# Two blocks on one core: all eight banks in one turn, ScalarE for the high parts of every dense weight unit, another place for the third FFN's second unit

## What is computed

```
for li in 0, 1:                                   # first block, two layers
    z = rms(x) @ w_in                              # 7756 columns: an mLSTM, a top-k attention, a differential attention
    merged = sum over 3 branches of sigmoid(gate) * (y_branch @ w_branch)
    x = x + merged @ w_out                         # 1024 x 1024
    x = x + (silu(rms(x) @ w_gate) * (rms(x) @ w_up)) @ w_down        # hidden 2816: first and second FFN
x = x + retention(rms(x) @ ret_w_in) @ ret_w_out   # ret_w_out: 2048 x 1024
x = x + (silu(rms(x) @ w_gate) * (rms(x) @ w_up)) @ w_down            # hidden 3584: third FFN
x = x + conv(rms(x) @ conv_w_in) @ conv_w_out
x = x + sum over 8 experts of gate_e * FFN_e(rms(x))                  # top 2 of 8, hidden 3584 each
out = rms(x) * g
```

## Time and profile before

| what | us |
|---|---|
| three runs | 2657.6, 2659.8, 2660.11 (median 2659.8) |
| the profiled execution | 2658.11 |
| its span, first to last instruction | 2656.3 |
| TensorE matmuls busy | 2592.8 (98%) |
| VectorE busy | 1803.0 (68%) |
| ScalarE busy | 1226.1 (46%) |
| GpSimd busy | 218.8 (8%), all of it L2251 but for 0.2 |

### The profile page before, as it was taken

How to read it: one execution, slowest core, us unless ns; L and a number is a source line. 1 busy time by engine, 2 the same in 40 slices (tenths; PEclk the granted TensorE clock), 3 DMA queues, 4 the chain that set the end, 5 groups by cost and what they waited for, 6 DMA issues and landing times.

```text
span 2656.3 us, 29239 instructions
## 1 busy us (share of the span) xinstructions
PE 2592.8 (98%) x11620; PEld 1989.4 (75%) x11620; DVE 1803.0 (68%) x1953; ACT 1226.1 (46%) x1423; POOL 218.8 (8%) x104
## 2 busy tenths in 40 slices
PE   8999999999999999999999998999999999999997
PEld 5455578865555888977788897878787888888886
DVE  3754555447445554745655567999999999999996
ACT  2233220023323102363100346777787877777775
POOL 0000023200000332000433100000000000000000
PEclk9999999999999999999999998999999999999999
DMA  6342455534334555545555455999999989999995
GB/s 214 129 154 100 158 192 189 170 110 137 127 113 170 193 190 173 184 157 175 175 190 190 143 176 181 375 325 381 320 379 325 377 324 376 325 355 347 354 345 188
DMA packets 273636, 610.13 MB, mean 230 GB/s; under 512 B 10476, under 2 KB 47522, under 8 KB 273338
## 3 DMA queue, kind: packets, MB, share of 16 engines
q1 hardware_dynamic: 273466, 607.67, 64.6%
HBM read 606.58 MB, written 1.05 MB: 229 GB/s over the span
## 4 chain that ended last, share of the span: by engine, by line
PE 90%; DVE 6%; ACT 3%; issue 1%; DMA 0%; SPq 0%; DVEq 0%; ACTq 0%
PE bank L467 87%; DVE split L1625 4%; PE bank L709 1%; PE bank L497 1%; ACT split L1195 1%; ACT parts L1195 0%; ACT xs L1195 0%; DVE tmp L1674 0%; DVE parts L1686 0%; ACT pbuf L1195 0%; DMA pbuf<-in_gain_rows 0%; DVE parts L1613 0%; ACT L1195 0%; ACT halves L1195 0%; DVE ybuf_tmp_high L1639 0%
## 5 line engine op out<-in xcount | busy, mean ns | idle before, releaser
L467 PE MATMUL bank<-split,parts 128*128 128x512 f32 (+1 forms) x6432 | 1463.3, 388 | 5.7 <-DVE split L1625 3.1
L467 PEld LDWEIGHTS bank<-split,parts 128*128 128x128 f32 x6432 | 1189.4, 188 | 247.3 <-issue 4.0
L1625 DVE TENSOR_TENSOR split<-ring,split 128x2048 fp32r<-128x2048 f32 x444 | 1020.4, 2344 | 81.9 <-POOL split L2251 60.9
L1195 ACT ACTIVATE split<-ring 128x2048 fp32r<-128x2048 f32 x344 | 659.6, 1921 | 187.0 <-PE bank L467 187.0
L467 PE MATMUL bank<-ring,xnT 128*128 128x512 f32 (+2 forms) x896 | 367.6, 567 | 0.0
L2251 POOL TENSOR_SCALAR split<-ring 128x2048 fp32r<-128x2048 f32 x100 | 218.6, 2187 | 1265.2 <-PE bank L467 1035.9
L467 PEld LDWEIGHTS bank<-ring,xnT 128*128 128x128 f32 x896 | 169.4, 190 | 180.0 <-issue 178.9
L1195 ACT ACTIVATE parts<-bank 128x512 fp32r<-128x512 f32 x128 | 68.8, 590 | 327.4 <-PE bank L709 327.4
L1639 DVE TENSOR_TENSOR halves<-ring,halves 128x1024 fp32r<-128x1024 f32 x96 | 116.4, 1224 | 84.1 <-ACT halves L1195 83.5
L1195 ACT ACTIVATE halves<-ring 128x1024 fp32r<-128x1024 f32 x96 | 101.3, 1059 | 153.9 <-PE bank L467 153.9
L1686 DVE TENSOR_TENSOR parts<-bank,parts 128x512 fp32r<-128x512 f32 x128 | 82.4, 686 | 124.9 <-ACT parts L1195 124.9
(11 more groups left out here) (260 smaller groups left out, 1861.1 us busy)
## 6 DMA issues: line engine op xcount, KB each, us to landing
ring<-in_moe_w_gate SPq DMA_DIRECT2D x112, 1024.0 KB, 8.0
ring<-in_moe_w_up SPq DMA_DIRECT2D x112, 1024.0 KB, 7.5
ring<-in_moe_w_down SPq DMA_DIRECT2D x112, 1024.0 KB, 7.5
ring<-in_w_gate_up SPq DMA_DIRECT2D x44, 1024.0 KB, 5.8
ring<-in_w_in SPq DMA_DIRECT2D x40, 1024.0 KB, 7.1
ring<-in_ret_w_in SPq DMA_DIRECT2D x24, 1024.0 KB, 5.1
ring<-in_w_down SPq DMA_DIRECT2D x22, 1024.0 KB, 5.1
ring<-in_w_in SPq DMA_DIRECT2D x20, 880.0 KB, 6.5
```

The lines of the kernel that those rows point to most:

```text
L467: return nc.tensor.matmul(o, l, r, start=first, stop=final, **kw)
L1195: return nc.scalar.activation(out, in_, func, **kw)
L1625: V.tensor_tensor(split[:, split_place(m), 1, :], ring[:, n % RING, :], split[:, split_place(m), 0, :].bitcast(F32), ALU.subtract).then_in ...
```

## The change

- ScalarE makes every high part, in `ffn_act`, in a written order: before a group's SiLU as many as the gate's units free, after it as many as the group's other units free. GpSimd's program goes.
- In the layers the early high and low parts follow 2, 1, 1 halves, the fourth unit last.
- In the third FFN and the experts the places are 3, 0, 1, 2 in turn. The third FFN's second unit thus goes where the first two of the retention's last four halves lay; it waits for these two and is made before the product ends. VectorE makes its low part between the addition of x's second half and the low parts of that half. Halves after the third FFN are numbered two places on.
- `to_x_split`, the transposes around it and the second filler take their banks from `ALL`; afterwards `LOW`'s counter is set so that the gate's banks aren't those emptied last.
- The last `combine` is preceded by a filler of three.

```diff
@@ split_place
-            return (3, 2, 0, 1)[(m - (DEPTH * layer_splits if m < dense_splits else dense_splits)) % SPLITS]
+            return (3, 0, 1, 2)[(m - (DEPTH * layer_splits if m < dense_splits else dense_splits)) % SPLITS]
@@ halves: place of half h
+            return (h if h < LAYER_HALVES + RET_HALVES else h + 2) % HALVES
@@ norm_transposes, input_split
-                filler(1)
+                filler(1, ALL)
@@ turn_residual
-                turn_input(x, (2 * h, 2 * h + 1), HIGH)
+                turn_input(x, (2 * h, 2 * h + 1), HIGH if h else ALL)
@@ to_x_split
-                bs = [fill(LOW) for _ in range(4)]
+                bs = [fill(ALL) for _ in range(4)]
...
+                for start in LOW:
+                    if bs[2] not in (LOW * 2)[start:start + 2] and bs[3] not in (LOW * 2)[start:start + 2]:
+                        turn[LOW] = start
@@ turn_merged; turn_o likewise
-                    turn_input(xs, (2 * h, 2 * h + 1), HIGH if h else ALL)
+                    turn_input(xs, (2 * h, 2 * h + 1))
@@ combine
+                filler(3 if ends else 0, LOW)
@@ ffn_act
                 highs(gain, pairs=(2, 3))
+                highs_to(SPLITS)
                 roots(xsum[:, 2, :], xsum[:, 1, :])
                 eng.wait_ge(rstd_dve.sem, act.next(rstd_dve))
-                for i in range(len(groups) + 1):
+                read = 0
+                for i in range(len(groups)):
                     if i:
-                        hidden_high(groups[i - 1][1], i == len(groups))
-                    if i < len(groups):
-                        gated(groups[i][1], normed=False)
+                        hidden_high(groups[i - 1][1], False)
+                    highs_to(read + ups[i] + SPLITS)
+                    gated(groups[i][1], normed=False)
+                    read += 2 * ups[i] + (downs[i - 1] if i else 0)
+                    highs_to(read - (1 if i + 1 == len(groups) else 0) + SPLITS)
+                hidden_high(groups[-1][1], True)
@@ layer, ScalarE (VectorE the same with half_lows and weights_low)
-                for _ in range(EARLY):
-                    half_highs(1)
+                for n in (2, 1, 1):
+                    half_highs(n)
                     expert_high(1, layer_splits * li)
+                expert_high(EARLY - 3, layer_splits * li)
@@ third FFN, ScalarE
             half_highs(8)
+            expert_high(1, first)
+            for h in range(LAYER_HALVES + RET_HALVES - HALVES, LAYER_HALVES + RET_HALVES - 2):
+                sig, value = half_read[h]
+                eng.wait_ge(sig.sem, value)
+            expert_high(1, first)
             ffn_act(groups2, G_FFN0, first)
@@ third FFN, VectorE
             weights_low(1)
-            to_ffn(G_FFN0)
-            weights_low(1)
+            to_ffn(G_FFN0, 1)
@@ to_ffn
                     add_to_x(BY_HALF[2 * h:2 * h + 2])
+                    weights_low(units if h else 0)
                     lows(gain, pairs=(2 * h, 2 * h + 1))
@@ GpSimd
-                    nc.gpsimd.tensor_scalar(split[:, split_place(m), 0, :], ring[:, n % RING, :], 1.0, 0.0, ALU.mult,
-                                            ALU.add).then_inc(high_made.sem, high_made.tick())
```

More of the change, by code:

```diff
@@ L46 @@
 LAYER_HALVES = DEPTH * KT
+RET_HALVES = 8 * 2 + 8 * 4 + 2 * KT
 EARLY = 4
@@ L344, in place_half @@
             else:
-                whole = [halves[:, h % HALVES, i, :] for i in range(2)]
+                whole = [halves[:, half_place(h), i, :] for i in range(2)]
             return [w.rearrange("p (k c) -> p k c", k=KT) for w in whole] if by_column else whole
@@ L499, in transposes, with filler @@
                 last_bank[0] = b
-            def filler(products):
+            def filler(products, pool):
                 if products:
-                    b = fill(LOW)
+                    b = fill(pool)
                     for _ in range(products):
@@ L509, in norm_transposes @@
             def norm_transposes(late=False, idle=(0, 0)):
-                filler(idle[0])
+                filler(idle[0], LOW)
                 if not late:
@@ L520, in norm_transposes @@
                                "act" if kp % 2 == 0 else "dve")
-                filler(idle[1])
+                filler(idle[1], ALL)
             def give_low(b):
@@ L535, in input_split @@
             def input_split():
-                filler(5)
+                filler(5, LOW)
                 eng.wait_ge(xs_act.sem, pe.next(xs_act))
@@ L1055, in o_ready @@
                 if k == 4:
-                    turn_o(RH - 1, HIGH)
+                    turn_o(RH - 1)
                     point("o turned")
@@ L1300, in hidden_high, with ffn_act, highs_to @@
                          view=lambda b: b[:, 0:n].rearrange("p (f t) -> p f t", t=P))
-            def ffn_act(groups, gain):
+            def ffn_act(groups, gain, first):
+                ups = [group_units(i, groups)[0] for i in range(len(groups))]
+                downs = [n // 256 for _, n in groups]
+                total = units_of(groups)
+                def highs_to(count):
+                    count = first + min(count, total)
+                    expert_high(max(0, count - nth_split[0]), first)
                 highs(gain, pairs=(0, 1))
@@ L1662, in add_to_x, with to_ffn @@
                 eng.wait_ge(dve_freed.sem, dve.latest(dve_freed))
-            def to_ffn(gain):
+            def to_ffn(gain, units=0):
                 for h in range(2):
                     add_to_x(BY_HALF[2 * h:2 * h + 2])
+                    weights_low(units if h else 0)
                     lows(gain, pairs=(2 * h, 2 * h + 1))
@@ L2053, in layer @@
                 half_lows(1)
-                for _ in range(4):
-                    half_lows(1)
+                for n in (2, 1, 1):
+                    half_lows(n)
                     weights_low(1)
+                weights_low(EARLY - 3)
                 to_ffn(G_FFN + 8 * li)
```

50 lines of the change are left out of this document (11 added, 39 removed).

## The result

| what | before | after |
|---|---|---|
| runs | median 2659.95, 2657.6 to 2660.31, four | median 2642.34, 2642.04 to 2644.26, four |
| the profiled execution | 2658.11 | 2644.26 |
| its span | 2656.3 | 2642.5 |

The ratio is 0.9939, interval 0.9924 to 0.9953: faster by 16 us (12.5 to 20). The profiled pair differs by 13.9 us, since the profiled execution of before lay 1.8 us under its median and that of after 1.9 us over its own.

A forecast was written before the change was run, and what follows sets the result against it. TensorE's matmuls are busy 98% of the span, leaving some 63 us and low-clock time to win. Terms 1.9 + 0.7 + 3.5 + 0.4 + 3.9 + 1.7 = 12.1 us took the median from 2659.8 to 2647.7; range 2644 to 2653.

The forecast's parts named there:

- layer 0: First layer: a bank wait of 1.2 us goes and the order 2, 1, 1 brings 0.7; gain 1.9 us.
- layer 1: Second layer: the order 2, 1, 1 removes the wait for the last half's low part; gain 0.7 us.
- the retention: Retention's product to x: other banks remove TensorE's 3.53 us wait for VectorE's `oT_low`; gain 3.5 us.
- the third FFN's start: Second unit made earlier: its 3.13 us wait and low clock go, a 0.9 us wait at the third remains; gain 3.9.
- the last filler: End of kernel: three filler products in TensorE's 2.59 us wait keep the clock full for the last matmuls; gain 1.7 us.
- The bank turn: Product to x on banks emptied earlier: gains 1.2 us in layer 0, 3.5 in the retention, 0.4 at the convolution's input.
- Places: Convolution's third and fourth half wait for the third FFN's last unit, experts' second place is free as late: cost 0.
- GpSimd's work on ScalarE: cost 0: Dense groups: 100 high parts of 1.92 us move to ScalarE, covered by 21.8 and 10.9 us; otherwise 1.2 us a group.
- the clock doesn't follow the waits: Rival: short low-clock stretches at the third FFN's start and the end remain, losing 1.7 + 1.7 us: 2651.1; chance 0.13.
- ScalarE in order: Rival: high parts ahead of `hidden_high` or the SiLU delay TensorE 1.2 us in each of 19 dense groups: 2670.5; chance 0.04.
- The third FFN's start stays as late: Rival: the early second unit brings nothing, the 3.13 us stall moves to unit three with its low clock: 2651.6; chance 0.09.
- VectorE holds the products: Rival: in both layers and the retention bank waits become waits for halves, losing 1.2 + 1.4 + 3.5 us: 2653.8; chance 0.06.

The follow-up runs named there:

- the kernel with one high part before the root: Changed kernel with one high part instead of two between the turned x and the square root in the third FFN: median 2642.22 us, ratio 0.9940.
- the bank turn alone: Kernel before with only the product to x, its transposes and the second filler on all banks, and `LOW`'s start set: median 2651.84 us, ratio 0.9975.
- the two conflicts alone: Changed kernel with the convolution's product to x on banks 0, 1, 5 and 6, so two old bank waits return: median 2647.38 us, ratio 0.9955.
- second profile of before: Kernel before, unchanged, run again with a profile of its own: median 2659.35 us, ratio 1.0004; the profiled execution took 2665.7 us.

## Why the prediction was wrong

Seven of its steps held: layer 0 (1.9 predicted, 2.08 in the ledger), layer 1 (0.7 and 0.70), the retention (3.5 and 3.58), the input's filler (0.4 and 0.53), the third FFN's start (3.9 and 4.04, with a wait of 0.77 us at the third unit where 0.9 was predicted), the last filler (1.7 and 1.68), and TensorE's waits for high parts in wide groups, which stayed away. It was the place and not ScalarE's speed that brought the third FFN's gain, as the prediction argued (3.5 of the 4.0 us). The load of the table took 1.28 us and the next instruction began 0.01 us later, and 0.02 in the kernel with one high part before the root. The row of the load that the prediction showed could not tell this, since 5.35 us of idleness lie behind it; earlier loads in the same trace could (at 58.89 us, for one, the next instruction starts 0.01 us after the load). The Trainium skill (ScalarE: Activation LUTs, What ACT_TABLE_LOAD costs) gives a switch 2.66 us with a drain; by an estimate from that the wait would have been 2.3 us, and the chain disagrees: no gap of 1.38 us stands before or behind the load.

Three steps failed.

**The list of what the bank turn touches was short.** Under "The bank turn" the prediction goes through layer 0, the retention and the convolution's input, and under "Places" it puts the convolution at 0. `to_x_split` runs a fourth time, in the convolution, and takes its banks from `LOW` there as well. The search went by TensorE's longest waits, 3.5 and 3.1 us; the two of 0.94 and 0.88 us stood in the same view's tail and were not looked for. The term, put at nothing, measured 2.3 us: the bank turn alone brings it, and the two conflicts alone take 2.12 of it away (1.82 of waits, the rest the overlap of neighbouring matmuls that a wait undoes). With this term the sum is 14.4, less than the distance of the medians still. Without these 2.3 us the time would have been 2644.6, inside the range.

**"GpSimd's work on ScalarE: cost 0".** The slack of 21.8 and 10.9 us was worked out for groups of 512. The layers' last group has 256 columns and one gate unit; there a high part in front of the hidden rows makes VectorE's low part late by 0.25 us. Cost: 0.5 us in all, not 0 and not 1.2 a group.

**The clock was taken as it stood in one profile.** It was called full but for three places; the pace of the first products, half up to 20.4 us, was not seen. The sum moved the low stretch of the third FFN (1.7 us) like a wait, and the retention's wait had none, from which the prediction drew that the clock doesn't fall there. The second profile of before has it the other way round. The changed kernel has neither wait, and neither stretch was seen without its wait: none of the nine profiles without the third FFN's old wait has one there, none of the twelve with the bank turn has one at the retention's. The distance of the medians was 14.8 and 17.6 us in two comparisons with a ledger of 14.4; a range whose lower end allowed 1.7 us of clock and 1 us of spread for all of this, on a sum that was 2.3 us short, didn't hold 2642.3. That the clock accounts for all of the remaining 0.4 and 3.2 us isn't shown: only one execution in each comparison was profiled, and the mean clocks on record, good to a thousandth of it, point that way but are too coarse, and are missing for the first comparison's executions of before.

Of the rivals, "the clock doesn't follow the waits" had its doubt borne out by the second profile of before, but not its price: no low stretch was left in either place. "ScalarE in order" was right in its mechanism in two groups of nineteen, at a fifth of the price. "The third FFN's start stays as late" and "VectorE holds the products" did not come.

## What to carry to other kernels

- When a shared helper changes, list every call of it and read the trace at each; don't start from the longest waits. The four waits under 1 us, two in the layers and two in the convolution, were worth as much here (3.7 us) as one of 3.5.
- When one engine takes over another's work in a written order, work the slack out for the smallest group, not for the usual one.
- A wait costs its length every time and its low clock sometimes. Put the first in the sum and the second in the range, and take two profiles of the kernel before if its runs spread by more than the terms. Read the pace of the matmuls beside the printed clock where a trace begins. A few products of constants in a stretch where TensorE waits for others can be worth more than the waits: 4.1 us at the routing.

## What the runs showed of the hardware

- **The clock behind a wait differs from execution to execution.** Retention, after waits of 3.53 and 3.69 us: full once, low for 6.8 us once. Third FFN, after 2.6 to 3.1 us: low for 3.4 us in four profiles, full in one. The end, after 2.59 us: low in all three profiles without the filler, in none with it. What decides it, no run here shows.
- **It also falls without a wait.** Stretches of 10.24 us at the half clock lie shortly before 206.7 in two profiles and near 720 in two, in dense work of small matmuls, in the kernel before and in changed ones, each some 3.7 us of time. In most profiles both places are at full clock. Why, no run here shows.
- **The first products run at half the pace until the clock records begin.** One starts every 0.427 us up to 20.4 us and every 0.216 after in the first profile of before; in seven others, whose records begin before the first product, all but the first of them come at 0.216. The 1.00 printed for the time ahead of the records is no reading.
- **Of a low part on VectorE and a high part on GpSimd that overlap, the second to start waits for the first.** In the kernel before 54 of the 444 low parts overlap a GpSimd high part. The 20 that begin while one is under way take 3.49 to 3.98 us (the third FFN's second unit in the earlier trace rows 3.71); the 34 that begin first take the usual 2.28 to 2.29, and GpSimd's high parts behind those take 2.36 to 3.99 us instead of 1.90. The low parts beside no high part have a mean of 2287 ns, all 444 of the changed kernel 2285. So the mean of 2344 mixes two kinds, and in dense work nobody waited for the long ones.
